# Fused two-block transformer: query norm from exponent bits, items and key spreads reordered, weight splits ahead of sums

## What is computed

```
q = (rms_norm(c_q, g_cq) @ w_uq).reshape(b, l, 8, 96)
q = rope_tail(rms_norm(q, g_q_mla), cos, sin)
k = rope_tail(rms_norm(k, g_k_mla), cos, sin)
o_mla = softmax(q k^T * 96**-0.5 + causal mask) v
h = h + concat(o_mla, o_fox) @ w_out
h = h + square(relu(rms_norm(h, g_mlp[0]) @ w_mlp_up[0])) @ w_mlp_down[0]
```

## Time and profile before

| what | value |
|---|---|
| median of three runs | 1332.41 us |
| the profiled execution, its own time | 1332.28 us |
| its span in the trace | 1330.5 us |
| TensorE busy | 1302.3 us |
| VectorE busy | 953.9 us |
| ScalarE busy | 743.5 us |
| POOL busy | 342.7 us |
| attention stage and output projection | about 95 to 175 us of the span |

### The profile page before, as it was taken

The page is one execution under the profiler, slowest core; times in us unless marked ns, Lnnn a source line. Parts: engine busy times, 40 slices in busy tenths (PEclk is TensorE's granted clock), DMA queues, the critical chain, the costliest instruction groups (busy, mean ns, idle before and its releaser), DMA issues. The chain is left out here.

```text
span 1330.5 us, 28216 instructions
## 1 busy us (share of the span) xinstructions
PE 1302.3 (98%) x10550; PEld 1274.0 (96%) x10550; DVE 953.9 (72%) x1426; ACT 743.5 (56%) x1192; POOL 342.7 (26%) x374
## 2 busy tenths in 40 slices
PE   9998999999999999999999999999999989999997
PEld 8987899999999999999899999999999989999996
DVE  6867787655487776655455669998559898999844
ACT  5555554444343554444556556666457886666542
POOL 4632133310011233200006214343103022434311
PEclk9999999999999999999999999999999999999998
DMA  9520155555555455555545545554564445555451
GB/s 307 187 100 1 67 188 190 189 191 180 174 185 188 159 190 189 190 187 177 205 158 186 190 155 199 188 182 147 186 214 173 169 167 198 205 183 180 158 191 55
DMA packets 35370, 230.50 MB, mean 173 GB/s; under 512 B 4062, under 2 KB 5214, under 8 KB 11910
## 3 DMA queue, kind: packets, MB, share of 16 engines
q1 hardware_dynamic: 34228, 226.99, 48.6%
q10 hardware_dynamic: 1058, 2.38, 0.5%
HBM read 228.17 MB, written 1.05 MB: 172 GB/s over the span
## 5 line engine op out<-in xcount | busy, mean ns | idle before, releaser
L392 DVE TENSOR_TENSOR wlo<-raw,whi 128x1024 fp32r<-128x1024 f32 (+1 forms) x446 | 525.5, 1182 | 104.7 <-ACT whi L386 102.2
L427 PE MATMUL ps<-xhi,whi 128*128 128x256 f32 (+2 forms) x1920 | 542.9, 283 | 4.9 <-DVE wlo L392 3.9
L428 PE MATMUL ps<-xlo,whi 128*128 128x256 f32 (+2 forms) x1920 | 542.0, 282 | 0.0
L429 PE MATMUL ps<-xhi,wlo 128*128 128x256 f32 (+2 forms) x1920 | 540.8, 282 | 0.0
L386 ACT ACTIVATE whi<-raw 128x1024 fp32r<-128x1024 f32 (+2 forms) x444 | 446.8, 1011 | 153.3 <-PE ps L429 135.7
L427 PEld LDWEIGHTS ps<-xhi,whi 128*128 128x128 f32 x1920 | 362.4, 189 | 8.6 <-issue 5.6
L429 PEld LDWEIGHTS ps<-xhi,wlo 128*128 128x128 f32 x1920 | 362.9, 189 | 0.0
L428 PEld LDWEIGHTS ps<-xlo,whi 128*128 128x128 f32 x1920 | 360.7, 188 | 0.3
L427 PE MATMUL ps<-hhi,whi 128*128 128x256 f32 (+1 forms) x1184 | 334.3, 282 | 2.0 <-issue 0.8
L429 PE MATMUL ps<-hhi,wlo 128*128 128x256 f32 (+1 forms) x1184 | 333.2, 281 | 0.0
L428 PE MATMUL ps<-hlo,whi 128*128 128x256 f32 (+1 forms) x1184 | 333.0, 281 | 0.0
(11 more groups left out here) (339 smaller groups left out, 1338.1 us busy)
## 6 DMA issues: line engine op xcount, KB each, us to landing
raw<-w SPq DMA_DIRECT2D x182, 1024.0 KB, 4.9
raw<-w SPq DMA_DIRECT2D x40, 768.0 KB, 4.2
raw<-w SPq DMA_DIRECT2D x4, 512.0 KB, 5.4
h<-x_fm ACTq DMA_DIRECT2D x4, 272.0 KB, 5.6
out_fm<-h SPq DMA_DIRECT2D x6, 128.0 KB, 1.9
ws<-ws_src ACTq DMA_DIRECT2D x1, 512.0 KB, 3.5
bs<-bs_rows ACTq DMA_DIRECT2D x1, 512.0 KB, 5.0
consts<-constants SPq DMA_DIRECT2D x1, 508.0 KB, 10.4
```

The costliest lines, as they stand in the source:

```text
L392: nc.vector.tensor_tensor(wlo[:, w, 0:n], raw[:, slot, col:col + n], whi[:, w, 0:n].bitcast(F32), ALU.subtract).then_inc(wlo_done, 3 if fr ...
L427: nc.tensor.matmul(o, hi, xh, start=start, stop=False)
L428: nc.tensor.matmul(o, hi, xl, start=False, stop=False)
L429: mm = nc.tensor.matmul(o, lo, xh, start=False, stop=stop)
```

## The change

Five edits:

1. `items`: the second halo item moves behind the first MLA head, from index 9 to 10. The reduction in `peak` moves with it.
2. `KEY_SPREAD` and `KEY_FINAL`: the last key pair moves from stage 7 to 8, and in each stage the spread stands behind `values` rather than ahead of `turn`. `q_stats` runs one turn sooner: parts 2 and 3 both in turn 3, part 4 in turn 4.
3. `query_power` leaves ScalarE. VectorE makes the inverse root by shifting and subtracting the number's bits and two Newton steps, eight instructions that each wait for the one before, in stage 7. POOL's step behind it stays.
4. Of `dve_log_sigmoid` only the two instructions ahead of the exponential stay in front of the output projection. The rest, and the two scalings, go behind `mlp0_up`.
5. In `attn_out` alone, VectorE splits unit j+3 ahead of the sum of tile j and no longer behind it. ScalarE's list is not changed.

```diff
@@ -544,6 +545,8 @@
                 for j in range(UB):
                     if j % segs != segs - 1:
                         ahead(dve, split_lo, p, it, j, last)
+                    if p.name == "attn_out":
+                        ahead(dve, split_lo, p, it, j, last)
                     if j % segs == segs - 1:
                         jt = j // segs
                         kt = it * per + jt
@@ -551,7 +554,8 @@
                         hh = h[:, kt, c0:c0 + t]
                         nc.vector.tensor_tensor(hh, ps[:, jt % ring + (4 - ring), 0:t], hh,
                                                 ALU.add).then_inc(tile_free, 1)
-                        ahead(dve, split_lo, p, it, j, last)
+                        if p.name != "attn_out":
+                            ahead(dve, split_lo, p, it, j, last)
                         if n != 8:
                             dve_xlo(dve, n, kt, c0, t)
             loop_peeled(dve, p.bodies, body)
@@ -809,14 +813,14 @@
         NHD = len(heads)
 
 
-        items = ([("d", 0)] + [("h", i) for i in range(HEADS)] + [("d", 1)]
-                 + [("h", HEADS + i) for i in range(HEADS)])
+        items = ([("d", 0)] + [("h", i) for i in range(HEADS + 1)] + [("d", 1)]
+                 + [("h", HEADS + i) for i in range(1, HEADS)])
         NIT = len(items)
         LATE_HI = {12: U_Q + 1, 14: U_Q + 2, 16: U_Q + 3}
         LATE_LO = {14: U_Q + 1, 16: U_Q + 2, 18: U_Q + 3}
         D1 = items.index(("d", 1))
-        KEY_SPREAD = {5: 1, 6: 2, 7: 3}
-        KEY_FINAL = {4: 0, 5: 1, 6: 2, 7: 3}
+        KEY_SPREAD = {5: 1, 6: 2, 8: 3}
+        KEY_FINAL = {4: 0, 5: 1, 6: 2, 8: 3}
         Q_PARTS = [(0, range(-1, 3)), (0, range(3, 6)), (1, range(-1, 3)), (1, range(3, 6)), (2, range(-1, 6))]
         item_of = {i: j for j, (kind, i) in enumerate(items) if kind == "h"}
 
@@ -1154,9 +1158,9 @@
                 if j == 1:
                     freed, n = tile_left(TL_Q + 5)
                     pe.wait_ge(freed, n)
-                if 1 <= j < 6:
-                    q_stats(j - 1)
-                if j == 6:
+                for part in {1: (0,), 2: (1,), 3: (2, 3), 4: (4,)}.get(j, ()):
+                    q_stats(part)
+                if j == 5:
                     pe.wait_ge(s("q_stats_out"), 2)
                 if kind == "d":
                     nc.tensor.transpose(ps[0:META, 6, 0:META], pr, ident[0:META, 0:META]).then_inc(pt_ps, 1)
@@ -1234,12 +1238,12 @@
             for st in range(4, NIT + 3):
                 if st < NIT:
                     scores(st)
-                if st in KEY_SPREAD:
-                    key_spread(KEY_SPREAD[st])
                 if st < NIT + 2:
                     turn(st - 2)
                 if items[st - 3][0] == "h":
                     values(items[st - 3][1])
+                if st in KEY_SPREAD:
+                    key_spread(KEY_SPREAD[st])
                 if st >= NIT:
                     j = st - NIT
                     if j < 2:
@@ -1458,6 +1462,24 @@
                 nc.vector.tensor_tensor(k_mla[64:96, 2 * i + o, :], k_rot[r, :], ps[r, bank, 0:T0],
                                         ALU.mult).then_inc(k_out, 1)
 
+            def query_power():
+
+                c, y, z, mean = s("q_power"), q_inv[:, :, :], q_neg[:, :, :], q_part[:, 0:3, :]
+                yi = y.bitcast(I32)
+                dve.wait_ge(s("q_mean"), 1)
+                nc.vector.tensor_scalar(yi, mean.bitcast(I32), 1, None, ALU.logical_shift_right).then_inc(c, 1)
+                dve.wait_ge(c, 1)
+                nc.vector.tensor_scalar(yi, yi, -1, 0x5F3759DF, ALU.mult, ALU.add).then_inc(c, 1)
+                for k in range(2):
+                    dve.wait_ge(c, 3 * k + 2)
+                    nc.vector.tensor_tensor(z, y, y, ALU.mult).then_inc(c, 1)
+                    dve.wait_ge(c, 3 * k + 3)
+                    nc.vector.scalar_tensor_tensor(out=z, in0=z, scalar=-0.5, in1=mean, op0=ALU.mult,
+                                                   op1=ALU.mult).then_inc(c, 1)
+                    dve.wait_ge(c, 3 * k + 4)
+                    nc.vector.scalar_tensor_tensor(out=y, in0=z, scalar=1.5, in1=y, op0=ALU.add,
+                                                   op1=ALU.mult).then_inc(c, 1)
+
             def peak(j):
                 kind, i = items[j]
                 b, sf = j % 2, soft[:, j % 2, :, :]
@@ -1469,6 +1491,7 @@
                 dve.wait_ge(mx_done, parts_done(j + 1))
                 if j == 1 + HEADS:
                     dve.wait_ge(q_scale, 6)
+                if j == D1:
                     nc.vector.tensor_reduce(q_d[0:META, 0:1], q_diag[0:META, :], AX.X, ALU.add).then_inc(q_scale, 1)
                     dve.wait_ge(q_scale, 7)
                     nc.vector.tensor_scalar(q_d[0:META, 1:2], q_d[0:META, 0:1], -1.0, None, ALU.mult).then_inc(q_scale, 1)
@@ -1508,6 +1531,8 @@
                     peak(st)
                 if 1 <= st <= NIT:
                     normal(st - 1)
+                if st == 7:
+                    query_power()
                 if st in KEY_FINAL:
                     k_normed(KEY_FINAL[st], 0)
                     k_normed(KEY_FINAL[st], 1)
@@ -1605,16 +1630,18 @@
                     to(LATE_LO[st])
 
             dve.wait_ge(s("params_loaded"), 16)
-            for _ in dve_log_sigmoid(dve, par("lam", 0, NB), half_lam[:, :], tmp[:, 0, 0:NB], tmp[:, 1, 0:NB],
-                            tmp[:, 0, NB:2 * NB], s("lam_step"), s("lam_exp_asked"), s("lam_exp")):
+            lam = dve_log_sigmoid(dve, par("lam", 0, NB), half_lam[:, :], tmp[:, 0, 0:NB], tmp[:, 1, 0:NB],
+                            tmp[:, 0, NB:2 * NB], s("lam_step"), s("lam_exp_asked"), s("lam_exp"))
+            next(lam)
+
+            dve_residual(dve, ph["attn_out"], 1, 1, C1, T1)
+            dve_rstd(dve, 1, C1, T1, ph["mlp0_up"])
+            dve_mlp_up(dve, ph["mlp0_up"], C1, T1)
+            for _ in lam:
                 pass
             nc.vector.tensor_scalar(half_lam[:, :], tmp[:, 0, NB:2 * NB], 4.0, None, ALU.mult).then_inc(s("lam_done"), 1)
             nc.vector.tensor_scalar(par("b_b_a", 0, 2 * NB), par("b_b_a", 0, 2 * NB), 0.5, None,
                                     ALU.mult).then_inc(s("gate_bias_done"), 1)
-
-            dve_residual(dve, ph["attn_out"], 1, 1, C1, T1)
-            dve_rstd(dve, 1, C1, T1, ph["mlp0_up"])
-            dve_mlp_up(dve, ph["mlp0_up"], C1, T1)
             dve_residual(dve, ph["mlp0_down"], 4, 2, C1, T1)
             dve_rstd(dve, 2, C1, T1, ph["conv_in"])
 
@@ -1828,13 +1855,6 @@
                     split_hi(act, rnd, (j + LA) % UB, 1 if done[0] + LA == p.units - 1 else 8, first=rnd == 0)
                     done[0] += 1
 
-            def query_power():
-
-                act.wait_ge(s("q_mean"), 1)
-                nc.scalar.activation(q_neg[:, :, :], q_part[:, 0:3, :], ACT.Ln).then_inc(s("q_log"), 1)
-                act.wait_ge(s("q_log"), 1)
-                nc.scalar.activation(q_inv[:, :, :], q_neg[:, :, :], ACT.Exp, scale=-0.5).then_inc(s("q_power"), 1)
-
             def roots(n):
                 act.wait_ge(n_ss, n + 1)
                 if n >= 2:
@@ -1902,7 +1922,7 @@
                 if second(j):
                     nc.scalar.activation(prob_0[0:3 * META, i // 2 % 2, HALO:T1], ps[0:3 * META, 6, 0:2 * P],
                                          ACT.Copy).then_inc(pt0_done, 1)
-                if j == 5:
+                if j == 4:
                     nc.scalar.activation(q_part[:, :, :], ps[:, 6, 2 * P:2 * P + 4 * HEADS].rearrange(
                         "p (t h) -> p t h", t=4), ACT.Copy).then_inc(s("q_stats_out"), 1)
                     nc.scalar.activation(q_inv[0:META, 2, :], ps[0:META, 6, 2 * P + 4 * HEADS:2 * P + 5 * HEADS],
@@ -1924,8 +1944,6 @@
                     exps(st)
                 if 2 <= st < NIT + 2:
                     turned(st - 2)
-                if st == 7:
-                    query_power()
                 if st >= 3 and second(st - 3) and items[st - 3][1] < HEADS:
                     high(items[st - 3][1] // 2)
             for t in range(N_TL):
@@ -2269,7 +2287,7 @@
             mean = q_part[:, 0:3, :]
             nc.gpsimd.tensor_scalar(mean, q_inv[:, :, :], 1.0 / QK, EPS ** 3, ALU.mult, ALU.add).then_inc(s("q_mean"), 1)
             c, scale, y, z = q_scale, QK ** -0.5, q_inv[:, :, :], q_neg[:, :, :]
-            pool.wait_ge(s("q_power"), 1)
+            pool.wait_ge(s("q_power"), 8)
             nc.gpsimd.tensor_tensor(z, y, y, ALU.mult).then_inc(c, 1)
             pool.wait_ge(c, 1)
             nc.gpsimd.tensor_tensor(z, z, mean, ALU.mult).then_inc(c, 1)
```

More of the change, by code:

```diff
@@ L20 @@
 F32R = mybir.dt.float32r
+I32 = mybir.dt.int32
 ACT = mybir.ActivationFunctionType
```

## The result

The changed kernel takes 1337.61 us (median of seven runs, 1336.49 to 1339.29) against 1332.41 us before (median of seven runs too, 1330.17 to 1333.31): ratio 1.0043, 95% interval 1.0031 to 1.0054. It is slower by 0.43%. A second series gave 1.0034 (1.0022 to 1.0046).

What follows compares the result with a forecast made beforehand. TensorE, busy 98% of the span, was taken as the bound. From 1332.28 us, attention's 2.5 was subtracted, 5.9 for the output projection and 1.4 for the clock added: 1337.1, or 1337.2 as median; range 1333.2 to 1339.6.

Steps and rivals of the forecast that it cites:

- a ring of 3.38 us: Output projection: each sum waits through VectorE's split and ScalarE's high part and square for the sum before, 3.38 us a step.
- a loss of 5.9 us: First up projection: xlo(7) ends at 183.4 us against 177.5 before, 5.9 us lost, bounds -1.9 and 6.5.
- 1.4 for the clock: First up projection: TensorE's clock is cut after idle time, costing 1.4 us, between 0 and 1.7.
- rival B: Output projection: the loop of waits does not bind and the 1.86 us gap closes: 1328.0 us, chance 0.13.
- A: Output projection: the loop of waits holds but the clock is not cut: 1335.8 us, chance 0.20.
- C: Attention gains less than 1 us, since VectorE's eight instructions and POOL's polish replace the table loads: 1339.6 us, chance 0.07.
- D: Attention gains its full 4.5 us and the clock is not cut: 1333.8 us, chance 0.10.
- the slack: Down projection: its fourth split has 4.9 us to spare against 3.1 us of delay by the moved log-sigmoid, so no cost.
- 2.5 us: Attention stage: the three attention changes together end it 2.5 us earlier, bounds 1.0 and 4.5.
- the three idle times: Attention: VectorE's waits of 1.88 (scores), 1.07 (second halo item's factors) and 1.60 us (scores at 131.10) counted as removed.
- 1.5 for the spreads: Attention, key spreads behind values: VectorE's wait of 1.88 us falls to 0.4, gain 1.5 us, between 0 and 1.88.
- 1.07 + 1.60 - 1.7 for norm and halo: Attention: two VectorE waits, 1.07 and 1.60 us, go, while the norm's eight VectorE instructions cost 1.7 us.

Runs made afterwards that it cites:

- e4: Changed kernel with 18 unused matmuls put ahead of each of TensorE's waits for xlo(6) and xlo(7): ratio 1.0017 to the kernel before.
- e6: Changed kernel with ScalarE's square of tile j put behind its high part of unit j+4 in the output projection: ratio 1.0017 to the kernel before.
- e5: Changed kernel with ScalarE making its high parts one unit further ahead in the output projection: ratio 1.0016 to the kernel before.
- e3: Changed kernel with VectorE's split ahead of the sum in step 0 of the output projection only: 1328.77 us, ratio 0.9967 to the kernel before.
- e1: Changed kernel with VectorE's split back behind the sum in the output projection: 1329.01 us, ratio 0.9967 to the kernel before.
- edit 4 alone: Kernel before with only the rest of the log-sigmoid moved behind the first up projection: ratio 0.9995.
- edits 1 to 3: Kernel before with only the three attention changes (key spreads and query statistics, query norm on VectorE, halo item): ratio 0.998.
- edit 2: Kernel before with only the query norm moved to VectorE, its eight instructions behind the last key's finish: ratio 1.0013.
- edits 1 and 3: Kernel before with key spreads behind values, earlier query statistics and the halo item moved, but the query norm still on ScalarE: ratio 1.0008.
- edits 1 and 2: Kernel before with the key spread and query statistics change and the query norm on VectorE, but the halo item not moved: ratio 1.0006.
- e2: Kernel before with only VectorE's split put ahead of the sum in the output projection: 1341.51 us, ratio 1.0061.

## Why the prediction was right, and where it was not

**Edit 5, the step that decides.** I had a ring of 3.38 us; it is 3.40 to 3.41. I had sum 7 at 181.5 and xlo(7) at 183.4; they are at 181.81 and 183.30 on an axis that ends attention 0.06 us later. I had a loss of 5.9 us and 1.4 for the clock, 7.3 together; the hand-over grew by 40.49 - 33.19 = 7.30. e4 gives the clock's part as 1.5 and leaves 5.8. The end of xlo(7) agrees by two errors that cancel: sum 7 came 0.3 us later, and xlo took 0.49 us where I had 0.87. The rival B (1328.0, the ring does not bind) is out by e6, where one instruction out of the ring moves the sums by its 0.31 us; A (no cut of the clock) is out by the clock's own row, 0.50 from 180 us; C and D (attention gives under 1 or 4.5) by the table: 2.0 and 3.6.
What I said of the mechanism was incomplete. I compared the ring with TensorE's 2.89 us a unit. e5 shows that this is not the measure. Half a microsecond behind the first sum TensorE has finished three units (in e3 it starts the fourth at 155.56, the first sum stands at 155.04). There the up projection starts at 170.20 and comes to its eighth block, the one for xlo(7), 2.5 later: 17.7 us behind the first sum. VectorE must make up that lead. In the new order seven steps and 1.5 us lie between the first sum and the end of xlo(7), so a step may take 16.2 / 7 = 2.3 us, and not 2.89. At 3.40 a step xlo(7) comes 7 x 3.40 + 1.5 = 25.3 us behind the first sum, 7.6 late; at 3.09, 23.1, 5.4 late; in e5, 21.5 + 1.5 = 23.0, 5.3 late. e3's own xlo(7) is 0.1 late (172.83). With 1.5 us of clock the hand-overs should exceed e3's by 9.0, 6.8 and 6.7 us. They do by 9.1 (40.49), 7.3 (38.76) and 6.8 (38.18); the 0.5 of e6 is the longer part of its slow stretch behind xlo(7), and e5's cut of 3.4 us lies behind xlo(7) whole. So even a step of 2.9 us would have lost, by the same sum an estimate of 4 us.

**Edit 4.** Right: e1 and edit 4 alone show the gap at 0.9 us, no wait at the new place. The first and the last instruction of the moved part there:

```profile
276.99 0.98 DVE L730 TENSOR_SCALAR tmp<-half_lam 128x12 f32<-128x12 f32 x1
...
280.82 0.17 DVE L1643 TENSOR_SCALAR params<-params 128x24 f32<-128x24 f32 x1
```

280.99 - 276.99 = 4.0 us rather than 3.1, the first of them 0.98 us long, and the slack covers it. The slack was 4.9 us by my sum; its parts give 268.3 for the start of the down projection where I wrote 268.0, and the trace of before has 267.86, which changes nothing.

**Attention.** I had 2.5 us. The profiled pair shows 2.0, the other seven traces with edits 1 to 3 show 3.6, and the medians of edits 1 to 3 alone 0.2% or 2.7 us. The range held, the terms did not, and that their sum came near is in part luck. VectorE's waits between 100 and 140 us sum to 8.8 us before and to 3.3 in the second trace of the changed kernel: 5.5 less, of which the eight instructions take 1.7. Of the three idle times that I counted as gone, 4.55 us, only 3.2 went: 1.88 fell to 0.27, 1.07 to 0, but 1.60 only to 1.12. The other 2.3 us came from waits that I had not counted, the largest this one of before, which is gone after:

```profile
125.67 0.65 DVE L1468 TENSOR_REDUCE soft<-ps 128x1 f32<-128x144 f32 x2 [1.36 <-PE ps L1142]
```

I also added the terms as if each stood alone: 1.5 for the spreads, 1.07 + 1.60 - 1.7 for norm and halo. Alone, by one trace each, edit 2 costs 0.75 us of attention, edits 1 and 3 cost 1.8, edits 1 and 2 gain 0.3; together the three gain 3.6 where the clock is not cut. The failing step is "I count it as gone with ScalarE's delay": an idle time is only gone if nothing else is late at that place. The wait for the keys (3.25 us in front of the halo item) is hidden by the move of the halo item, and this move pays only with the norm off ScalarE, whose load of 3 us otherwise stands before the first MLA head.
A part of attention's gain is the clock, and its size stays open. The four kernels with the old place of the spreads (before, edit 4, edit 2, e2) all show a cut that begins between 104 and 109 us, so the old order was never seen without one: against e2 the gain is 2.1 us, against before 3.6. Of the ten kernels and traces with the new place two show a cut there: the changed kernel's first trace (55.1 us in place of 53.4) and edits 1 and 3. I had written that cut into the hand-over only.

**The clock in the hand-over.** Right in sign and size. The page of the Trainium skill that I named (TensorE: Matmul & The Clock Gate, Why this matters for your kernels) warns of idle gaps between bursts of matmuls, and the traces agree in that: the half rate began at 180.0, right behind the first of the two waits of 2.4 us, and its 6.8 us were worth 1.5 us of time. The gap of 1.86 us was followed by a cut of 3.4 us in two of the five traces that have it (edits 1 to 3; edits 1 and 2), each worth 1.5 us too. What decides between a cut and none is not shown; the changed kernel itself has a cut in attention in one trace and not in the other.
On table loads the sum went by the trace, 1.28 us and no drain, and the case with the loads kept (edits 1 and 3) again has the next activation 1.29 us behind the load.

## What to carry to other kernels

Before moving an instruction ahead of another in one engine's list, follow what it waits for through the other engines' lists until you are back at the first one, or not: if you come back, the parts no longer overlap but add up to a period. Compare that period not with the consumer's but with what it takes to make up the lead that the consumer has. And where a late start is the trouble, change the first step alone (here 0.84 us in the trace, too little to show in the medians).

## What the hardware showed that I had not expected

VectorE's xlo takes 0.49 us in the changed kernel's output projection and 0.87 in before's, and the low split takes 1.23 in the changed kernel and 1.68 in e5. What differs is when POOL's sum of squares starts. In before it starts 0.11 us ahead of xlo (160.35), in the changed kernel 0.36 us behind it (159.01):

```profile
160.24 0.70 POOL L534 TENSOR_TENSOR ssum<-ssum,sq 128x258 f32<-128x258 f32 x1 [16.19 <-ACT sq L515]
...
159.37 0.64 POOL L535 TENSOR_TENSOR ssum<-ssum,sq 128x258 f32<-128x258 f32 x1 [15.27 <-ACT sq L516]
```

That POOL works beside is not enough. In the trace of before, 182 low splits beside which POOL starts later take 1.2 us like those without POOL. The slow ones start while a sum, product or difference of POOL runs, and take what is left of it plus a fixed time, 1.08 us for a split and 0.28 for xlo: 0.60 + 1.08 = 1.68 (e5), 0.30 + 1.08 = 1.38 (where a difference of POOL ends at 270.69), 0.59 + 0.28 = 0.87. So the earlier trace rows's 0.87 is a property of the order of the two starts, not of the instruction, and the change made xlo shorter without helping.
The clock cut lands on different waits in different kernels, and moves attention by 1.7 us (53.4 against 55.1, the same kernel) and the hand-over by 1.5, more than several of the edits are worth.
